# Hybrid attention layers: the value products of three branches issued one loop step later

## What is computed

```python
for l in range(DEPTH):                       # DEPTH = 2
    h = ffn(h, 0)
    u = rms_norm(h, g[2]) * (1 + scale) + shift
    # A: differential attention, 4 pairs of heads        B: 2-D neighbourhood attention, 8 heads
    # C: grouped queries with normed q and k, 8 heads     D: sliding window with a sink, 8 heads
    acc = sum(sigmoid(u @ w_gate[i]) * (branch_i(u) @ w_branch[i]) for i in range(4))
    h = h + gate * rms_norm(acc @ w_out, g[3])
    h = ffn(h, 2)

def attend(q, k, v):
    p = softmax(q @ k.T / 8)                 # per head, 64 wide
    return p @ v
```

## Time and profile before

| | us |
|---|---|
| median of 3 runs | 2534.37 (2529.94 to 2536.66) |
| the profiled execution's own time | 2532.3 |
| its span | 2530.5 |
| PE busy in the span | 2428.9 |
| DVE busy | 1581.3 |
| ACT busy | 1064.8 |
| granted clock of TensorE, mean | 0.988 |

### The profile page before, as it was taken

How to read it: one execution, slowest core, us unless ns; L and a number is a source line. 1 busy time by engine, 2 the same in 40 slices (tenths; PEclk the granted TensorE clock), 3 DMA queues, 4 the chain that set the end, 5 groups by cost and what they waited for, 6 DMA issues and landing times.

```text
span 2530.5 us, 31850 instructions
## 1 busy us (share of the span) xinstructions
PE 2428.9 (96%) x12584; PEld 1973.4 (78%) x12584; DVE 1581.3 (62%) x2620; ACT 1064.8 (42%) x1842; POOL 27.4 (1%) x43
## 2 busy tenths in 40 slices
PE   6999998999999999989999989999989999988998
PEld 3888886877767676768888868888868788778998
DVE  2798888355455557688887874333355456588654
ACT  5222235355454535462222342222354555556444
POOL 0000000000000000000000000000000000000000
PEclk9999999999999999999999999999999999999999
DMA  5556554321322112225655523322234243233554
GB/s 234 184 207 216 187 178 159 95 76 63 104 71 71 63 67 84 71 88 192 210 206 191 186 99 108 100 99 85 96 113 141 76 142 121 88 125 126 185 178 154
DMA packets 98069, 331.42 MB, mean 131 GB/s; under 512 B 11009, under 2 KB 12033, under 8 KB 97281
## 3 DMA queue, kind: packets, MB, share of 16 engines
q1 hardware_dynamic: 97922, 329.39, 38.4%
HBM read 323.06 MB, written 6.29 MB: 130 GB/s over the span
## 4 chain that ended last, share of the span: by engine, by line
PE 90%; DVE 4%; ACT 3%; issue 1%; DMA 1%; SPq 0%; POOL 0%; DVEq 0%; ACTq 0%
PE ps L347 26%; PE ps L338 24%; PE ps L339 24%; PE ps L649 5%; PE ps L1180 3%; PE ps L1155 3%; PE ps L1165 3%; DVE w_low L327 1%; ACT w_high L321 1%; ACT prob L1304 0%; PE ps L548 0%; DMA mod_first<-in_mods 0%; DVE stat L1464 0%; PE ps L1124 0%; ACT pt L1314 0%
## 5 line engine op out<-in xcount | busy, mean ns | idle before, releaser
L327 DVE TENSOR_TENSOR w_low<-raw,w_high 128x1024 fp32r<-128x1024 f32 (+1 forms) x488 | 551.7, 1136 | 495.3 <-ACT w_high L321 494.5
L321 ACT ACTIVATE w_high<-raw 128x1024 fp32r<-128x1024 f32 (+1 forms) x488 | 481.6, 990 | 762.1 <-DMA raw<-in_weights 761.9
L338 PE MATMUL ps<-u_high,w_high 128*128 128x512 f32 (+1 forms) x2208 | 771.0, 361 | 4.2 <-DVE acc L1421 1.4
L339 PE MATMUL ps<-u_low,w_high 128*128 128x512 f32 (+1 forms) x2208 | 762.6, 357 | 0.0
L347 PE MATMUL ps<-u_high,w_low 128*128 128x512 f32 (+1 forms) x2496 | 542.9, 362 | 4.8 <-DVE w_low L327 4.8
L347 PEld LDWEIGHTS ps<-u_high,w_low 128*128 128x128 f32 x2496 | 422.5, 190 | 91.6 <-issue 19.7
L338 PEld LDWEIGHTS ps<-u_high,w_high 128*128 128x128 f32 x2208 | 418.8, 190 | 89.4 <-issue 17.1
L339 PEld LDWEIGHTS ps<-u_low,w_high 128*128 128x128 f32 x2208 | 418.9, 190 | 58.1
L410 DVE CUSTOM_DVE_ANT_0 ps<-mod_raw,c_all,smalls 128x1024 f32<-128x1024 f32 x256 | 319.5, 1290 | 2.2 <-DMA mod_raw<-in_mods 1.7
L338 PE MATMUL ps<-hid_high,w_high 128*128 128x512 f32 (+1 forms) x704 | 249.0, 362 | 0.0
L339 PE MATMUL ps<-hid_low,w_high 128*128 128x512 f32 (+1 forms) x704 | 249.0, 362 | 0.0
(11 more groups left out here) (151 smaller groups left out, 2258.5 us busy)
## 6 DMA issues: line engine op xcount, KB each, us to landing
raw<-in_weights SPq DMA_DIRECT2D x360, 512.0 KB, 3.5
mod_raw<-in_mods SPq DMA_DIRECT2D x128, 512.0 KB, 4.2
raw<-in_weights SPq DMA_DIRECT2D x64, 384.0 KB, 3.1
raw<-in_weights SPq DMA_DIRECT2D x64, 320.0 KB, 2.9
mod_first<-in_mods SPq DMA_DIRECT2D x16, 512.0 KB, 13.1
h_kept<-h SPq DMA_DIRECT2D x16, 256.0 KB, 2.0
na_bias<-in_na_rows SPq DMA_DIRECT2D x16, 256.0 KB, 4.0
h<-h_kept SPq DMA_DIRECT2D x2, 2048.0 KB, 8.0
```

Source lines behind the costliest of these rows:

```text
L321: act.activation(w_high[s][:, 0:width], raw[s][:, 0:width], ACT.Copy).then_inc(high_made.sem, 1)
L327: dve.tensor_tensor(w_low[s][:, 0:width], raw[s][:, 0:width], w_high[s][:, 0:width], ALU.subtract).then_inc(low_made.sem, 1)
L338: pe.matmul(o, w_high[s][:, w], x_high(x), start=first and a == 0, stop=False)
L339: pe.matmul(o, w_high[s][:, w], x_low(x), start=False, stop=False)
```

## The change

In B, C and D `mix(p)`, `high_of_out(p)` and `low_of_out(p)` go from step 2p+2 to step 2p+3. In branch A they stay. The last pair stays behind the loop. No instruction is added or removed; in each loop the pairs but the last one move: 7 in each branch of layer 0, 3 in each of layer 1, 30 in all.

```diff
@@ tensor
-                    if j % 2 == 0 and j:
-                        mix(j // 2 - 1)
+                    for p in self.mixes(j):
+                        mix(p)
                     flip(j)
@@ scalar
                     keep_probs(j)
-                    if j % 2 == 0 and j:
-                        high_of_out(j // 2 - 1)
+                    for p in self.mixes(j):
+                        high_of_out(p)
@@ new
+            def mixes(self, j):
+
+                after = 2 if self.b == "A" else 3
+                return [p for p in range(self.NP - 1) if 2 * p + after == j]
@@ vector
-                    elif j % 2 == 0 and j:
-                        low_of_out(j // 2 - 1)
+                    else:
+                        for p in self.mixes(j):
+                            low_of_out(p)
```

## The result

The changed kernel takes 2538.37 us (median of 20 runs, 2536.52 to 2543.74), the kernel before 2532.11 us in 20 runs beside it: ratio 1.0023, 95% interval 1.0016 to 1.0030. It is 0.23% slower, within the 0.3% of "no change that can be told" but clear of zero. Forecast were 2537.6 us in a range of 2530.5 to 2543.0, by a growth of 3.2 us; the growth is 5.8 us by the ratio (4.1 to 7.6 by its interval) and 6.1 us between the two profiled spans. That 2537.6 lies within 1 us of the result is luck: the median of 3 runs that it started from, 2534.37, was 2.3 us above that of the 20, and the growth worked out was too small by 2.6 us.

What follows compares the result with a forecast made beforehand. PE, busy 96% of the span, was taken as the bound. Terms 2 x (0.60 + 0.73) - 0.55 + 0 + 0.27 + 0.83 gave +3.2 us on the 2534.37 median: 2537.6 us, range 2530.5 to 2543.0.

Steps and rivals of the forecast that it cites:

- The bound, and where the change acts: Whole kernel: PE busy 96% of the span, so the total moves only by PE's waits or its instructions' cost elsewhere.
- No cost in the loops up to step 13 in B0, C0 and B1: Up to step 13 of these loops, high or low parts cover the moved products' absence: no waits, cost 0.
- 13 high in B0 and C0: Step 14: 13 high newly waits for ACT's copy of 12, behind a moved result copy; +0.6 us each.
- The ends, 0.73 each: Ends of B0, C0, D0, D1: last products also wait for the single bank, behind NP-2's high and low parts; +0.73 us each.
- D0, -0.55: D of layer 0: waits of 0.56, 0.57, 0.78 go; 0.53, 0.10 and the end's 0.73 come; -0.55 us.
- C1, +0.27: C of layer 1: 12 high waits longer for ACT's copy of 11, behind pair 1's result copy; +0.27 us.
- D1, +0.83: D of layer 1: 7 high starts 1.8 us earlier, then 1.9 us of products, +0.1; end +0.73; +0.83 us in all.
- The sum, +3.2: All loop terms together, no cost assumed for changed neighbours: +3.2 us, 0.13% slower; chance 0.68.
- No net effect: Rival: ends and new wait may cost nothing while waits in D0 and D1 go; 2531.8 to 2535 us, chance 0.17.
- The ends lower the clock: Rival: longer waits at four loop ends each bring a slow-clock stretch of 1.7 us; 2544.5 us, chance 0.07.
- Late copies everywhere: Rival: each of the 30 moved result copies on ACT gets in PE's way, 0.27 us each; 2545 us, chance 0.04.
- broad gains: Rival: later products cover most of the six loops' 18.5 idle us; about 2526 us or below, chance 0.04.

Runs made afterwards that it cites:

- third: Kernel before, with only pair NP-2 one step later in B, C and D, 6 moves of 30; ratio 1.0025 to the kernel before.
- fourth experiment: Changed kernel, with the last pair's products in PSUM bank 0, free by then, instead of the single bank; ratio 1.0011 to the kernel before.
- same order: Code of the change with the step put back to 2p+2, so every engine's program is the one of before; ratio 1.0005 to the kernel before.
- last pair stays: Changed kernel, but pair NP-2 stays in its old step, leaving 24 of 30 moves; ratio 1.0006 to the kernel before.
- two steps later: Kernel before, with pairs in B, C and D moved two steps instead of one, NP-2 in the last step; ratio 1.0022 to the kernel before.
- chosen places: Kernel before, with all pairs but pair 1 one step later only in D0, last products in a free bank; ratio 1.0003 to the kernel before.
- 2 repeats: Kernel before, with the first scores of B0 computed 2 times more, nothing else changed; ratio 0.9997 to the kernel before.
- 4 repeats: Kernel before, with the first scores of B0 computed 4 times more, nothing else changed; ratio 1.0007 to the kernel before.

## Why the prediction was right, and where it was off

**The bound, and where the change acts**: right. PE's chain is 90% in both kernels, and 3.89 of the 4.15 us by which the loops grew is idle time of PE.

**No cost in the loops up to step 13 in B0, C0 and B1**: right in that no wait came. From the first scores to `flip(13)` B0 takes 87.87 us, 87.94 before. B1 is 0.17 us longer in all, without a listed wait: perhaps the changed neighbours, for which I had left -3 to +3 us open over the 30 moves, perhaps the correction.

**13 high in B0 and C0**: right in mechanism and size. By `flip(15)` B0 had grown 777.99 - 680.52 less 777.50 - 680.70, 0.67 us, for the 0.60 worked out (0.50 of it is listed as a wait). The third and fourth experiment show its two halves apart from the end wait.

**The ends, 0.73 each**: right in mechanism, small in size. Each of the four waits grew by 0.82 or 0.83. What was missing is the release: PE starts 0.05 us behind ACT's copy (778.74 to 778.79) but 0.14 us behind DVE's subtraction (780.02 to 780.16). I had used 0.05 for both. That is not so behind every operation of DVE: at the wait of 1.96 us in B1 its last one ends at 2067.58, and PE starts at 2067.63. Why these ends take longer stays open.

**D0, -0.55**: -0.51 less slow clock. The waits went and came where they were put: new 0.54 for 0.53; 0.56, 0.57 and 0.78 gone. The small wait of 0.1 in step 10 is not listed.

**C1, +0.27**: the wait grew by 0.25, the loop by 0.14.

**D1, +0.83**: the term that was most mis-sized, 1.16 less slow clock, 1.22 in the rows. The wait of 7 high grew by 0.49 us, beside which the loop up to `flip(7)` grew by 0.34. What I had left out lies ahead of them: `keep_probs(5)`, with which this row of work on ACT begins, starts as `flip(5)` ends. First before, then after:

```profile
2265.06 1.04 PE L1165 MATMUL ps<-smalls,prob 128*128 128x128 f32 x8
...
2266.13 1.03 ACT L1314 ACTIVATE pt<-ps 128x1024 f32<-128x1024 f32 x1
```

```profile
2268.61 1.10 PE L1165 MATMUL ps<-smalls,prob 128*128 128x128 f32 x8
...
2269.75 1.03 ACT L1314 ACTIVATE pt<-ps 128x1024 f32<-128x1024 f32 x1 [2.38 <-PE ps L1165]
```

Counted from the first scores of D1, `keep_probs(5)` starts at 35.63 instead of 35.44 us, 0.19 later, though PE has the same work ahead of `flip(5)`, in another order. With the 0.27 of the moved copy `exps(7)` ends 0.46 later; `keep_probs(6)`, the gate and 7 high follow it. Why `flip(5)` ends later is not shown: no wait is listed for it, and slow clock is less than 0.1 us of it. So 7 high starts 1.6 us earlier, not 1.8.

**The sum, +3.2**: 4.07 in the loops, 0.2 more than worked out in each of B0, C0 and B1, 0.3 in D1, 0.1 less in C1. The other 2 us are no term of the sum: 1.45 behind D1, 0.64 between D0 and B1, -0.14 in all the rest. Between these two executions they are the clock. Behind D1, at a wait of 2.50 us that is as long in both kernels, only the changed one shows a slow stretch, whose price is 4.0 x (1 - 0.57) = 1.7 us:

```profile
2300.00:2304.00 4.00, 3.96 (x20) 3.96 (x21) 3.65 (x9) 1.54 (x3) 0.00 (x0) 0.57 0.08 32
```

The kernel before, where that wait ends at 2295.4:

```profile
2296.00:2300.00 4.00, 3.96 (x33) 3.72 (x32) 3.02 (x9) 2.19 (x4) 0.00 (x0) 1.00 0.00 0
```

Between D0 and B1, the slow stretch at 1116 us lasts some 3.4 us longer, but nearly all of that falls on a wait of 6.8 us that both kernels have there. Products behind that wait come 2.46 us later than before at first (1120.61 for 1118.15) and 2.82 us later behind the stretch (1127.39 for 1124.57); the other 0.3 us comes at the next two slow stretches, at 1491 and 1863 us.

That is one execution of each kernel. Over all runs, (1 - granted clock) x span averages 34.3 us for the changed kernel and 32.5 to 33.5 us for before beside the experiments, one to two us more: about the rest. The same average goes with what is left of the times of the other kernels once their loops are taken off:

| us, against the kernel before | growth by the ratio, less that of the loops | (1 - granted clock) x span, mean of the runs |
|---|---|---|
| same order | +1.2 | +0.2 |
| last pair stays | +0.6 | +1.8 |
| last pair only | +3.1 | +1.9 |
| last in free bank | +1.8 | +2.5 |
| two steps later | +1.5 | +0.2 |
| chosen places | +2.9 | +2.6 |
| 2 repeats | -2.5 | -2.6 |
| 4 repeats | -1.7 | -1.1 |

The first column is uncertain by some 2.3 us each way, so only three of its eight numbers are clear of zero (+3.1, +2.9, -2.5), and the second also counts slow clock that falls on waits. But the sign is the same in all eight: what the times hold beyond the loops goes with the clock. That such shifts come from the place in time alone is shown for one stretch, in D0. It was not shown for the others, nor that they do so in each run.

**The rivals.** "No net effect" fell with the order on ACT. "The ends lower the clock" fell in the place I gave it: behind the end waits of 1.51 and 1.94 us the clock stayed at 1.00 in this profile. But between the two profiled executions the clock is where 2 us went, at waits far behind. The Trainium skill, page "TensorE: Matmul & The Clock Gate", section "What's actually happening", calls the window over which the chip watches PE free-running: it does not start anew with the kernel. The stretches of D0 above agree with that: granted 0.66, 1.00 and 0.64 behind the same wait at three places in time. "Late copies everywhere" and "broad gains" did not come.

## What to carry to other kernels

Moving a product later lets it cover another wait, but the last one before the loop ends moves next to its successor: look there first, for a buffer that both use. Where an engine works in the order written, a moved small copy costs its own length only if a result with less slack stands behind it, so walk the slack of each result at the new place. And where the gain or loss is a few us, compare lengths of loops less their slow clock beside the whole times: one profile gave them to 0.1 us where the clock stayed up and to some 0.3 us where it fell.

## What the runs showed of the hardware that was not expected

One wait of 1.9 us ahead of the first transposes of D0 was followed by a granted clock of 0.66 over 4 us in the kernel before, of 1.00 where the same work stands 2 us later in time, and of 0.64 where it stands another 2 us later. A wait of 2.50 us behind D1 was followed by 1.00 before and 0.57 in the changed kernel. The stretch in D0 cost 1.6 us (76.60 against 75.00); for the others in these loops 1.6 to 1.7 us is an estimate from their clock. At the loop ends PE started 0.14 to 0.15 us behind the end of DVE's subtraction, where it had started 0.05 us behind ACT's copy; in B1 it started 0.05 us behind DVE too.
